# Expert rows added into the residual in memory by the scatter, and part of the output projection moved into HGRN2's last head

## The reference

```python
for layer in range(2):
    hn = rmsnorm(x, norm_mix[layer])
    if layer == 0:  x = x + concat(rwkv7(hn @ w_in), rglru(hn @ w_in)) @ ab_w_out
    else:           x = x + hgrn2(hn @ c_w_in) @ c_w_out      # 8 heads of 128 channels
    hn = rmsnorm(x, norm_ffn[layer])
    x = x + hier_moe(hn)
return rmsnorm(x, norm_final)

# hier_moe: per token the best of 4 groups, in it the best 2 of 8 experts
gates = g_gate * top_v / sum(top_v)                    # two gates per token
hid = silu(xb @ w_gate[e]) * (xb @ w_up[e])            # 1024 -> 512
ys  = hid @ w_down[e]                                  # 512 -> 1024
out = segment_sum(ys * row_gate, row_tok)              # two rows per token are added
```

## Time and profile before

| | us |
|---|---|
| median of 3 runs | 2790.54 (2790.24 to 2793.55) |
| the profiled execution, whole | 2791.1 |
| its span, first to last instruction | 2789.3 |
| PE busy | 2574.3 (92%) |
| PE weight loads busy | 2077.8 (74%) |
| DVE busy | 1913.4 (69%) |
| ACT busy | 1608.3 (58%) |
| POOL busy | 378.0 (14%) |

### The profile page before, as it was taken

How to read it: one execution, slowest core, us unless ns; L and a number is a source line. 1 busy time by engine, 2 the same in 40 slices (tenths; PEclk the granted TensorE clock), 3 DMA queues, 4 the chain that set the end, 5 groups by cost and what they waited for, 6 DMA issues and landing times. The chain is left out here.

```text
span 2789.3 us, 58868 instructions
## 1 busy us (share of the span) xinstructions
PE 2574.3 (92%) x21332; PEld 2077.8 (74%) x21332; DVE 1913.4 (69%) x2191; ACT 1608.3 (58%) x1874; POOL 378.0 (14%) x342
## 2 busy tenths in 40 slices
PE   6998899988979999999969999998797999999995
PEld 5776799946758888888748777776684888888882
DVE  5348356534469999999655676677436899999973
ACT  3656223243338888888635566556222788888872
POOL 0020000000003333333201000000000222222220
PEclk9999999988989999999979999999898999999997
DMA  4111000013259999999641111111324999999974
GB/s 114 38 38 31 27 4 4 4 62 116 102 182 368 379 384 383 381 374 380 239 192 31 39 37 35 39 32 47 123 76 156 362 377 380 383 382 383 380 275 194
DMA packets 219995, 525.45 MB, mean 188 GB/s; under 512 B 43824, under 2 KB 99120, under 8 KB 219824
## 3 DMA queue, kind: packets, MB, share of 16 engines
q1 hardware_dynamic: 201392, 489.34, 47.5%
q0 software_dynamic: 18432, 33.60, 3.2%
HBM read 506.06 MB, written 50.33 MB: 199 GB/s over the span
## 5 line engine op out<-in xcount | busy, mean ns | idle before, releaser
L1812 DVE TENSOR_TENSOR w_low<-w_raw,w_high 128x1024 fp32r<-128x1024 f32 x768 | 894.9, 1219 | 31.7 <-DVEq L52 22.0
L1490 ACT CAST w_high<-w_raw 128x1024 fp32r<-128x1024 f32 x768 | 755.4, 1049 | 109.7 <-ACTq L52 108.8
L1665 PE MATMUL ps<-w_high,x_high 128*128 128x512 f32 x1024 | 414.9, 405 | 7.0 <-PEq L52 6.1
L1669 PE MATMUL ps<-w_high,x_low 128*128 128x512 f32 x1024 | 403.9, 394 | 0.0
L1668 PE MATMUL ps<-w_low,x_high 128*128 128x512 f32 x1024 | 401.9, 392 | 0.0
L1665 PEld LDWEIGHTS ps<-w_high,x_high 128*128 128x128 f32 x1024 | 195.4, 191 | 50.3 <-issue 13.6
L1669 PEld LDWEIGHTS ps<-w_high,x_low 128*128 128x128 f32 x1024 | 194.1, 190 | 43.4
L1668 PEld LDWEIGHTS ps<-w_low,x_high 128*128 128x128 f32 x1024 | 194.9, 190 | 37.6
L1665 PE MATMUL ps<-w_high,hidden_high 128*128 128x512 f32 x512 | 200.9, 392 | 6.7 <-PEq L52 6.7
L1668 PE MATMUL ps<-w_low,hidden_high 128*128 128x512 f32 x512 | 200.4, 392 | 0.0
L1669 PE MATMUL ps<-w_high,hidden_low 128*128 128x512 f32 x512 | 200.4, 391 | 0.0
(11 more groups left out here) (428 smaller groups left out, 4941.2 us busy)
## 6 DMA issues: line engine op xcount, KB each, us to landing
w_raw<-in_moe_w_gate SPq DMA_DIRECT2D x256, 512.0 KB, 5.4
w_raw<-in_moe_w_up SPq DMA_DIRECT2D x256, 512.0 KB, 5.7
w_raw<-in_moe_w_down SPq DMA_DIRECT2D x256, 512.0 KB
w_raw<-expert_rows SPq DMA_DIRECT2D x32, 512.0 KB, 9.3
w_tiles<-in_c_w_in SPq DMA_DIRECT2D x28, 512.0 KB, 4.0
w_tiles<-in_ab_w_in SPq DMA_DIRECT2D x22, 512.0 KB, 3.8
residual<-in_x SPq DMA_DIRECT2D x16, 512.0 KB, 7.6
h_rows<-hn_moe SPq DMA_DIRECT2D x16, 512.0 KB, 2.9
```

The costliest lines, as they stand in the source:

```text
L1490: act.copy(wh[:, p, :], raw[:, p, :]).then_inc(high_made, 1)
L1665: ins = pe.matmul(ps[:, bank, :], high, w_h, start=first, stop=False)
L1669: return pe.matmul(ps[:, bank, :], low, w_h, start=False, stop=final)
L1812: dve.tensor_tensor(wl[:, p, :], raw[:, p, :], wh[:, p, :].bitcast(F32), ALU.subtract).then_inc(low_made, 1)
```

## The change

The scatter adds into the residual in memory. The residual tiles are stored to `c.res_rows` in the prologue, right behind each `hn` tile; the scatter names the token (`src_tok`) as its row and has `compute_op=add`; `c.ys` and `dst_row` go. The gate is multiplied in before the down product, so it must be known by row: PE places the gates by 16 more small matmuls, and `hidden` multiplies by a column of `gate_row`. In the tail `sum_rows` and `combine` go, and SP loads 8 tiles of the residual in place of 16 of `c.ys`. The gain's load moves up behind the first residual tile. Separately, in `hgrn`'s last head ACT and DVE split the first 7 heads' output of token tiles 0 and 1 and PE computes their products with `w_out` (84 matmuls) in place of most fillers, left in PSUM banks 0 to 3; `project(t, h)` in moe(1) then does only k = 7 for t = 0 and 1.

```diff
+        def first_row(t):
+            return KT - 1 if split is not None and t < 2 else 0
...
                 for k in range(KT):
-                    if not early and split is None:
-                        sp.dma_start(raw[:, k, :], w_out[k * P:(k + 1) * P, :]).then_inc(raw_in[k], 16)
                     if fetch is not None:
                         sp.dma_start(c.res[:, k, :], fetch[k * P:(k + 1) * P, :]).then_inc(res_in[k], 16)
-                sp.dma_start(gb, gain.partition_broadcast(P)).then_inc(gain_in, 16)
+                    if k == 0:
+                        sp.dma_start(gb, gain.partition_broadcast(P)).then_inc(gain_in, 16)
...
                     sp.dma_start(c.rows[t * P:(t + 1) * P, :], hn[:, t % 2, :]).then_inc(rows_in[t % 2], 16)
+                    sp.dma_start(c.res_rows[t * P:(t + 1) * P, :], c.res[:, t, :]).then_inc(kept, 16)
...
-                for i in range(2 * TT):
-                    t, k = i // 2, i % 2
-                    if i >= NPC:
-                        sp.wait_ge(used, i - NPC + 1)
-                    sp.dma_start(raw[:, i % NPC, :], c.ys[k * S + t * P:k * S + (t + 1) * P, :]).then_inc(raw_in[i % NPC], 16)
-                    if i == 1:
+                for t in range(TT):
+                    sp.dma_start(c.res[:, t, :], c.res_rows[t * P:(t + 1) * P, :]).then_inc(raw_in[t], 16)
+                    if t == 1:
                         sp.dma_start(gb2, next_gain.partition_broadcast(P)).then_inc(next_in, 16)
...
+                pool.wait_ge(kept, 16 * TT)
...
-                    pool.tensor_copy(idx[:, 1:2], dst_row[:, b]).then_inc(order_p, 1)
+                    pool.tensor_copy(idx[:, 1:2], src_tok[:, b]).then_inc(order_p, 1)
                     take(pool, order_p)
-                    pool.indirect_dma_start(c.ys, bass.IndirectOffsetOnAxis(ap=idx[:, 1:2], axis=0), yb, None,
-                                            bounds_check=2 * S - 1, oob_is_err=False).then_inc(arrival, 16)
+                    pool.indirect_dma_start(c.res_rows, bass.IndirectOffsetOnAxis(ap=idx[:, 1:2], axis=0), yb, None,
+                                            bounds_check=S - 1, oob_is_err=False, compute_op=ALU.add).then_inc(arrival, 16)
...
                 def next_square(t):
-                    act.wait_ge(combined, t + 1)
+                    take(act, raw_in[t], 16)
...
                 last.then_inc(placed, 1)
+                pe.wait_ge(gates_spread, 1)
+                for i in range(2 * TT):
+                    last = pe.matmul(ps[:, B_S, 0:NBLK], at_pos[:, i, :].bitcast(F32), at_gate[:, i, :], start=i == 0, stop=i == 2 * TT - 1)
+                last.then_inc(gates_placed, 1)
                 stay_warm(7)
...
-                    dve.tensor_tensor(hid, hid, ps[:, B_U, :], ALU.mult).then_inc(hid_ready, 1)
+                    dve.scalar_tensor_tensor(out=hid, in0=hid, scalar=gate_row[:, b], in1=ps[:, B_U, :], op0=ALU.mult,
+                                             op1=ALU.mult).then_inc(hid_ready, 1)
...
                 ch(dve.tensor_tensor(gate[:, 1, :], gate[:, 0, :], col["m2"], ALU.mult))
+                dve.tensor_tensor(at_gate, reach[:, :, 0:NBLK], bcast(gate[:].rearrange("p k t -> p (k t)"), 2, NBLK), ALU.mult).then_inc(gates_spread, 1)
                 low(gate_up[3:5])
...
-                ch(dve.tensor_copy(dst_row[:], dstf))
...
+                dve.wait_ge(gates_placed, 1)
+                ch(dve.tensor_copy(gate_row[:], ps[:, B_S, 0:NBLK]))
...
+                def out_products(ks, parts, first=False):
+                    for k in ks:
+                        pe.wait_ge(out_low if parts == (2,) else out_high, k + 1)
+                        for part in parts:
+                            for t in range(2):
+                                x = c.x_ahead[:, 2 * (part == 1) + t, 0, k * P:(k + 1) * P]
+                                w = (h_low if part == 2 else h_T)[:, k, :]
+                                for h in range(2):
+                                    pe.matmul(ps[:, 2 * t + h, :], x, w[:, h * HALF:(h + 1) * HALF], start=first and part == 0, stop=False)
...
+                        if not more and lv < 6:
+                            stay_busy()
+                        if not more and lv == 6:
+                            take(pe, bank_free[1])
+                            pe.wait_ge(x_low, 2)
+                            out_products((0,), (0, 1), first=True)
...
                     project(4)
+                    if not more:
+                        out_products((1,), (0, 1))
                     take(pe, s["v_rows_ready"])
...
                     project(8)
+                    if not more:
+                        out_products((2,), (0, 1))
                     take(pe, s["kd_rows_ready"])
...
                     project(8)
+                    if not more:
+                        out_products((3, 4), (0, 1))
                     take(pe, s["s_ready"])
...
                     project(4)
+                    if not more:
+                        out_products((5,), (0, 1))
                     take(pe, s["sq_ready"])
...
                     project(13)
+                    if not more:
+                        out_products((6,), (0, 1))
+                        out_products(range(7), (2,))
...
                     level_exp(3)
+                    if not more:
+                        take(act, s["head_done"])
+                        for t in range(2):
+                            act.copy(c.x_ahead[:, t, 0, 0:7 * P].rearrange("p (k n) -> p k n", k=7),
+                                     y_T[:, 0:7, t * P:(t + 1) * P]).then_inc(x_high, 1)
...
+                        if not more and lv in (4, 5):
+                            t = lv - 4
+                            dve.wait_ge(x_high, t + 1)
+                            high = c.x_ahead[:, t, 0, 0:7 * P].rearrange("p (k n) -> p k n", k=7)
+                            dve.tensor_tensor(c.x_ahead[:, 2 + t, 0, 0:7 * P].rearrange("p (k n) -> p k n", k=7),
+                                              y_T[:, 0:7, t * P:(t + 1) * P], high.bitcast(F32), ALU.subtract).then_inc(x_low, 1)
```

More of the change, by code:

```diff
@@ L1299, in moe @@
         prod, ex, ex2, oh1, oh2 = (at[n] for n in ("prod", "e_logits", "e_rest", "e_hot1", "e_hot2"))
-        sel, both, incl, rank, far, rsel = (at[n] for n in ("sel", "sel_both", "counts", "rank", "far", "rank_sel"))
+        both, incl, rank, far = (at[n] for n in ("sel_both", "counts", "rank", "far"))
+        sel, rsel = at["sel_rank"][:, 0:2], at["sel_rank"][:, 2:4]
+        at_gate = at["sel_rank"].rearrange("p a e t -> p (a e t)")[:, 0:2 * TT * NBLK].rearrange("p (i b) -> p i b", b=NBLK)
         cmp8, nblk, over, oend, jump = (at[n] for n in ("cmp_blocks", "n_blocks", "over", "over_end", "jump"))
@@ L1604, in project @@
                     for ys, wp, ready in ((xh, wo_h, wo_high), (xl, wo_h, None), (xh, wo_l, wo_low)):
-                        for k in range(KT):
+                        for k in range(first_row(t), KT):
                             if t == 0 and h == 0 and ready is not None and split is None:
@@ L1608, in project @@
                             ins = pe.matmul(ps[:, B_P + 2 * (t % 2) + h, :], ys[:, t % 2, k, :], wp[:, k, h * HALF:(h + 1) * HALF],
-                                            start=n == 0, stop=n == 3 * KT - 1)
+                                            start=n == 0 and first_row(t) == 0, stop=n == 3 * (KT - first_row(t)) - 1)
                             n += 1
@@ L1620, in next_turn @@
                     last.then_inc(next_turned, 1)
[L1622 to L1632, removed]
                 def turn_rows(t):
@@ L1752, in first_head @@
                     first_projection(pe, c, m, 0, h_high, h_low).then_inc(c.first_done, 1)
-                if last_norm:
+                if not last_norm:
                     for t in range(TT):
[L1756 to L1762, removed]
                         next_turn(t)
@@ L1827, in hidden_low, with step @@
                                       hh.rearrange("p k n -> p (k n)").bitcast(F32), ALU.subtract).then_inc(hl_ready, 1)
-                def step(q, last=False):
+                def step(q, b, last=False):
                     if not last:
@@ L1833, in step @@
                         low(range(2, 2 * GU))
-                    hidden()
+                    hidden(b)
                     low(down_p)
@@ L1931, in _ @@
                 x_low(0)
[L1932 to L1951, removed]
-                        last = dve.scalar_tensor_tensor(out=c.res[:, t, :], in0=raw[:, i % NPC, :], scalar=gate[:, k, t:t + 1],
-                                                        in1=c.res[:, t, :], op0=ALU.mult, op1=ALU.add)
-                        last.then_inc(used, 1)
-                    dve.wait_ge(used, 2 * t + 2)
-                    dve.sem_inc(combined, 1)
-                dve.tensor_tensor(scale_by, bcast(c.ident[:], 1, TT), bcast(gate[:, 0, :], 2, P), ALU.mult).then_inc(scales, 1)
```

(13 more changed lines are left out.)

38 lines of the change are left out of this document (13 added, 25 removed).

## The result

The changed kernel takes 2792.71 us (median of 12 runs), the kernel before 2790.09 beside it: ratio 1.0018, 95% interval 1.001 to 1.0026, slower by 0.2%. The forecast was 2746, which is faster. The profiled execution took 2792.9 us, its span is 2791.0. Nearly all that the two tails gave, the expert loop took back.

What follows compares the result with a forecast made beforehand. PE was taken to set the expert loop's pace, with 1.3 us of DMA room per block. Terms -19.8 - 22.4 + 2.4 + 0 + 2.0 - 0.5 - 6.5 = -44.8 took 2791.1 to 2746.3, forecast 2746 us (2738 to 2757).

Steps and rivals of the forecast that it cites:

- (c): Accumulating scatter: 0 in the expert loop, extra landing latency of 1.2 us in each tail, +2.4 us for both.
- Rival A: Expert loop: accumulating rows overload the DMA engines and weights come late, above 500 ns a row; chance 0.12.
- Rival D: Whole kernel: gain and loss cancel, with accumulating rows at 640 to 720 ns, 2790 us; chance 0.03.
- signs of being wrong: Longer blocks, the last scatter's landing over 5 us, or PE dense from the start of moe(1).
- (a): moe(0)'s tail: first rows at T + 5.4, further tiles 2.9 us apart, loads not binding; -19.8 us.
- (b): moe(1)'s tail: first rows at T + 5.4, then seven steps of 1.82 us; -22.4 us.
- T: In each tail, the time the first loaded tile is used, 3.70 us after SP's first load in moe(0).
- (d): Gates in planning: DVE product +0.75 us, 16 PE matmuls mostly covered by idle time; +1.0 a layer, +2.0 us.
- (f): moe(1)'s prologue: 84 matmuls go, 18 us of PE, but waits for first rows and router biases leave -6.5 us.
- (e): HGRN2's last head: DVE differences +2.2 us, outputs at the full clock about -2.5; term -0.5 us.
- the first rival: Rival A, overloaded DMA engines in the loop; at five plain rows' cost, 870 ns a row, 2839 us.

Runs made afterwards that it cites:

- run 3: Changed kernel with rows dealt in another order over both partition halves, chosen so the first 64 rows fall on 8 of 16 engines; 2791.5 us.
- run 2: Changed kernel with each block's rows dealt over all 16 DMA engines; 2749.9 us, ratio 0.986.
- Run 6: Kernel before with the output projection's part alone (HGRN2's last head, shorter start of moe(1)); 2790.8 us, ratio 1.0003.
- run 7: Kernel before with the output projection's part, plus the norm's gain row loaded behind the first residual tile; 2787.9 us, ratio 0.9991.
- run 1: Changed kernel with a plain scatter, the add in the DMA left out; 2747.0 us, ratio 0.985.

## Why the prediction was wrong

**Step (c), the loop, is the step that failed.** It set the accumulating rows' cost in the loop at nothing, since the 0.70 us of doubled rows was under "1.3 of room"; the two loops measured 40.5 us longer. The doubling was right (2 x 174 is near the 359 ns found). The room was not there. It came from two averages: 414 GB/s of all engines together against a block's bytes, and the extra spread over 16 engines. The valid rows of a block sit on half of them, by the Trainium skill's map given with run 3; runs 2 and 3 agree with it. These had 112 rows of 157 ns in 17.93 us, 0.3 us of room by this estimate; the other half has more, and the dips in the GB/s line that I read as a queue run dry do not show that the fullest engine rests too. The added 8 rows are 1.26 us on it, 0.3 are covered, and 0.9 a block is what the trace has. The weights' landing grows at first, 8.6 us (850 to 900), 12.0, then 13.8 (950 to 1000): the first blocks of each layer still keep 17.9. So the loops cost 19.6 + 20.9 = 40.5 us from the first gather on, of which 19.1 + 20.3 = 39.4 lie between first and last scatter. Run 2 gives back 42.8 by the medians; its profile has 38.2 of them between first and last scatter and 2.7 in the tails' landings.

Rival A named the place and the sign, but by the same average put its threshold at 500 ns a row. By the fullest engines it is 174 + 0.3 / 8 x 1000, about 212 ns. Rival D, gain and loss cancel, is the outcome that came; it had a chance of 0.03, since it asked for 640 to 720 ns a row where 359 were enough. Two of the prediction's own signs of being wrong came true: blocks got longer, and the last scatter's landing took over 5 us (6.4).

**Steps (a) and (b), the tails**, were right in mechanism: first square 3.4 after SP's load (said: 3.7), first rows at T + 5.6 in moe(0) and 5.8 in moe(1) (said: 5.4), then about 2.9 apart in moe(0) and, from the second on, 1.82 in moe(1). They gave 16.6 and 18.2; with the landing's 1.2 each, 18.6 and 21.2 were said. The mis-sized term is the accumulate's landing, 3.0 us more than before and not 1.2, twice; the next largest part, 1.2, is moe(1)'s second tile behind the gain row. "Loads do not bind" was wrong there, once.

**Step (d)**: +0.4 in moe(0) at the first gather, where +0.75 was said. The 16 float32 products did not stay under their cover. PE's time line of the changed kernel in moe(0)'s planning, answering:

```profile
801.39 1.11 PE L1640 MATMUL ps<-ident,x_rows 128*128 128x128 f32 x8
805.57 0.47 PE L1647 MATMUL ps<-w_high,x_high 128*128 128x512 f32 x1 [3.07 <-PEq L52]
```

The idle 3.01 before the turn of the gathered rows is gone and the turn starts 3.75 later; the step had allowed 0.6 to 4.2. The products behind it start at the full clock (0.47 here, 0.76 for the first one before), and at the first scatter, 848.86 against 848.85, with the phase 0.8 earlier, 0.8 is left; +1.0 was said. So the step was right in moe(0), with its reason. In moe(1) it cannot be told from (f).

**Step (e)**: +0.8 and not -0.5. The outputs run at 2.4 GHz, as said. Time lines of PE and DVE of the changed kernel, answering:

```profile
1962.76 1.84 DVE L2468 SCALAR_TENSOR_TENSOR states<-states,step_decay,ps 128x128 f32<-128x128 f32 x4 [0.16 <-DVEq L52]
...
1965.34 0.46 PE L2184 MATMUL ps<-scores_T,v_rows 128*128 128x128 f32 x2 [0.70 <-PEq L52]
1965.64 0.39 PE L2185 MATMUL ps<-q_from_start,states 128*128 128x128 f32 x2
```

HGRN2 itself starts 2.5 later than before. Counted from its start the states end 3.0 later, where 2.2 was said; pairs of outputs take 0.39 in place of 0.63, and 2.5 come back.

**Step (f)**: -4.4 at the first gather, -6.5 said; both waits and the low clock of `project(2,0)` were named. Run 6 shows what the step left out: without the gain row's new place, a small edit of the diff, nothing of this is left. The working used it ("rows of tile 0, about 11 us after the phase begins") and never named or priced it. At its first scatter the changed kernel still has 3.7 of the 4.4; run 7 kept about half there. Why they differ is open.

Of the Trainium skill's two rules, "Collectives: The Full Stack" (The bandwidth ceiling) has two source reads for one add, both on the same read ring. The row's doubled time agrees with it; the reads themselves no run shows (the page of the profile has 497.67 MB read from memory with the add and, in run 1, without it). The prediction drew the wrong thing from the rule: twice the traffic on a full engine is time. The Trainium skill's rule on accumulates behind one another ("DMA: Bandwidth & Descriptors", Two DMAs through the same engine are not ordered) was taken to speak against a long hold of the engine per row, and 359 ns, against the 870 of the first rival, agree.

The 46.6 us between 2746.3 and 2792.9 are then 40.5 of the loops, 5.0 of the tails, 1.8 of (d) to (f), less 0.8 by which moe(0) began earlier. Run 1's 2747.0 is near the forecast in part by luck: it has no accumulate's landing, for which the forecast had 2.4, and (d) to (f) gave less than forecast.

## What to carry to other kernels

Count the packets of the fullest DMA engine, not the mean. Here valid rows on the first 64 partitions or so acted as a load on half of the engines, and neither the busy share (0.99 before, 1.02 in run 2, both with a dense PE; 1.00 with a starving one) nor the GB/s (384 and 382) shows room. Where row order is free, deal the rows over the engines; it took one constant here, and was worth 43 us in all once the rows were heavier, and nothing before. When the kernel takes work from an engine's start, look up which loads stand ahead of the next input on the queue, for they inherit the wait.

## What the hardware showed unexpectedly

A row of 4 KB of an accumulating scatter takes 327 ns of a DMA engine in the median packet against 159 for a plain one (359 against 174 in the mean by shares of time). From the last scatter's issue to SP's next load it takes 6.4 us in both tails, against 3.36 and 4.1 for a plain one in run 1. Dealt over 16 engines (run 2) it took 4.6 in moe(1) (2710.62 to 2715.26) and 5.4 in moe(0) (1395.04 to 1400.48). A DMA share at or above 1.00 went with a dense PE and with a starved one alike.
